# S5 stage: state factors of all batches on VectorE, skip weights put into the inner matrices, turned outputs copied by ScalarE

## The chip, the cores and the metric

The kernel runs on one core of one Trainium2 chip. The metric is the device time of one launch in microseconds (us). A core has TensorE (PE; its weight loads are listed as PEld), VectorE (DVE), ScalarE (ACT), GpSimd (POOL) and SyncE (SP), each with its own instruction stream; the streams meet at semaphores. DMAs are issued here from SP and ScalarE, a few from GpSimd.

## The reference, cut to what matters

The program is two blocks in a row, 512 tokens of width 1024, all in fp32. The first block is a gated linear attention layer and an S5 layer, the second an attention layer with a sparse half and a gated MLP. The change is in the S5 layer:

```python
# s5 mixer, per group g of 16 channels, 64 complex states p
lam_bar = exp(lam * dt); b_bar = (lam_bar - 1) / lam * b
bu[l,g,p] = sum_i u[l,g,i] * b_bar[g,p,i]
states = associative_scan(state[l] = lam_bar * state[l-1] + bu[l])
y = real(states) @ c_re - imag(states) @ c_im
y = y + d_skip * u
y = gelu(y); y = y * sigmoid(y @ w_glu + b_glu); y = y * silu(z)
out = y @ w_out
```

There are 128 groups of 16 channels; u and z are 2048 wide. d_skip (input s5_d, shape 1 x 128 x 16) is the skip weight of every channel.

## The kernel before, in words

Every dense product is made of three TensorE products (high and low parts of weights and activations). The weights come in loads of 1 MB into a ring of three slots, issued by SP (line 2970); ScalarE writes the high part of a load (line 1507), GpSimd (line 2849) or, in the S5 stage, VectorE (`low_weights`, line 2131, "ring_lo") the low part. TensorE takes the tiles in one fixed order, and each engine's order is written out by hand in its own program (`pe_program`, `act_program`, `dve_program`, `pool_program`, `sp_program`).

The S5 layer runs from about 405 to 1000 us. Its scan part works in 16 batches of 8 groups, one after the other. The sequence of 512 tokens is cut in 64 blocks of TB = 8 steps. A batch b needs:

- Bn(b), the input factors, made by VectorE (`b_factors`, lines 2414 to 2417: three instructions on 128 x 1024 elements), which TensorE turns (`b_to_rows`, line 1030, in two halves through one PSUM bank) and ScalarE copies to WB (`b_rows`, line 1739);
- W1(b), the state factors, from the turned C (`c_to_columns`, `columns`, tile CZ). In batches 0 to 10 GpSimd makes them (lines 2889 to 2891), in batches 11 to 15 (`DVE_STATES`) VectorE (`state_factors`, lines 2427 to 2429), again three instructions on 128 x 1024;
- the inner matrix: TensorE's `inside` (line 1041) multiplies Bn and W1, ScalarE's `spread` (line 1747) copies the result to GS, 16 x 8 x 128. Eight DMAs (`inner_rows`, line 2944, by SP; for batch 0 by ScalarE itself, line 1755) lay GS out along the diagonal of KM, a 128 x 1024 matrix whose zeros GpSimd wrote once (line 2882);
- u by blocks: the tile of u goes to DRAM (`u_tile`) and comes back as UB (`u_loads`, eight DMAs by SP);
- TensorE's `additions` (line 1051) multiplies WB and UB, VectorE's `scan` (lines 2449 to 2463) runs the recurrence over the blocks to M;
- TensorE's `outputs` (lines 1062 and 1065) adds UB x KM and M x W1, ScalarE copies (`outputs_of`, line 1762), TensorE turns them back to features (`by_feature`, line 1078, into PA[:, 2]), and VectorE's `add_skip` (line 2403) adds d x u in place into U. ScalarE's `gelu` follows.

Beside each batch TensorE makes dense tiles (`BESIDE`): three in batches 0 to 7 (u and z), two in batches 8 to 15 (z, from batch 10 on the first half of the GLU product, `glu_a`). VectorE scales the u and z tiles (`scaled`, line 2471). In batch 9 VectorE also makes eight low parts of U (line 2080) behind ScalarE's eight high parts.

In the ScalarE program, before the loop over the batches, the order is: `rotations_of(0)`, `u_tile(2)`, `spread(0)` with the eight DMAs of KM[0], `u_tile(3)`; in the loop first `b_rows(b + 1, 0)`. TensorE's second `b_to_rows` of a batch waits until ScalarE has read the first half:

```python
1026:  pe.wait_ge(bf_ready, b + 1)
1027:  if b + h > 0:
1028:      pe.wait_ge(wb_sb, 2 * b + h)
```

SP's stream holds the ring loads and, between them, `inner_rows(b)`, `u_loads(b + 1)` and `factor_loads(b + 3)`, issued when the tile count has reached the batch.

## Time and profile before

| | |
|---|---|
| time, median of 3 runs | 1710.36 us (1709.78 to 1710.69) |
| profiled execution | 1707.65 us, of it the span 1705.8 us |
| mean granted TensorE clock | 0.995 of full speed |
| busy share of the span | PE 98%, PEld 79%, DVE 60%, ACT 40%, POOL 34% |
| chain that ended last, by engine | PE 89%, DVE 6%, ACT 2%, issue 1% |
| TensorE's waits in the S5 stage (420 to 810 us) | 8.1 us in 2 waits for VectorE's Bn; 4.5 us "issue" before outputs (line 1062); 0.3 us for ScalarE's WB |

The busy shares are averages over stages that have different limits. How to read the profile: the table by stretches tells which engine is full in a stretch; the timeline shows an engine's instructions in order, with start, duration, and in brackets the idle time before an instruction and what ended it. A row with "x2" merges instructions; overlapping ends of neighbours come from the pipelines, so the step from one start to the next is the cost in a chain. The profiled execution is 2.7 us below the median of the runs.

### The profile page before, as it was taken

The numbers are of one execution on the slowest core, as the hardware profiler recorded it, in microseconds if no ns is written. First come the engines' busy times: TensorE is split into PE (matmuls) and PEld (weight loads), VectorE is DVE, ScalarE is ACT, GpSimd is POOL, SyncE is SP. The second block draws the span as 40 slices with busy tenths as digits, with TensorE's granted clock in tenths as the row PEclk, the third lists the DMA queues.
The fourth block names the chain that finished last, engine by engine and source line by source line (L and its number), as shares of the span: only waits on it lengthen the run. The fifth ranks groups of instructions, "written<-read, shape, count | busy, mean of one in ns | idle before, by whom it ended". The sixth has DMA issues, their size and how long they took to land.

```text
span 1705.8 us, 23173 instructions
## 1 busy us (share of the span) xinstructions
PE 1672.4 (98%) x9339; PEld 1340.0 (79%) x9339; DVE 1026.0 (60%) x1536; ACT 675.9 (40%) x968; POOL 581.7 (34%) x202
## 2 busy tenths in 40 slices
PE   9999999999999998999999999999999999999998
PEld 7777788888888886777888887687677888887877
DVE  4356535677999999995462755898973222222123
ACT  4473323334443456445333332426673322222122
POOL 2231014343743342000244432233773433443442
PEclk9999999999999999999999999999999999999999
DMA  5232003335645454444744322112002333332322
GB/s 173 75 99 90 10 26 99 85 88 150 158 129 130 137 141 113 115 116 154 265 128 132 99 72 75 50 44 87 1 2 75 98 99 97 82 93 78 100 86 83
DMA packets 266239, 167.86 MB, mean 98 GB/s; under 512 B 88747, under 2 KB 246790, under 8 KB 266006
## 3 DMA queue, kind: packets, MB, share of 16 engines
q1 hardware_dynamic: 254528, 146.44, 30.6%
q10 hardware_dynamic: 11158, 18.08, 3.2%
q0 software_dynamic: 448, 1.88, 0.3%
q8 instruction: 74, 1.21, 0.3%
q14 instruction: 31, 0.25, 0.1%
HBM read 144.86 MB, written 16.78 MB: 95 GB/s over the span
## 4 chain that ended last, share of the span: by engine, by line
PE 89%; DVE 6%; ACT 2%; issue 1%; ACTq 0%; DMA 0%; POOL 0%; DVEq 0%; POOLq 0%
PE PS L726 25%; PE PS L727 24%; PE PS L728 24%; PE PA L1051 1%; PE PA L970 1%; PE PA L967 1%; PE PS L1356 1%; PE PA L944 1%; PE PS L1344 1%; PE PA L1078 1%; PE PA L1306 1%; PE PA L1062 1%; PE PA L1183 1%; DVE ring_lo L2131 1%; PE PS L1030 1%
## 5 line engine op out<-in xcount | busy, mean ns | idle before, releaser
L2849 POOL TENSOR_TENSOR ring_lo<-ring,ring_hi 128x2048 fp32r<-128x2048 f32 (+2 forms) x90 | 393.6, 4373 | 919.2 <-ACT ring_hi L1507 916.6
L1507 ACT ACTIVATE ring_hi<-ring 128x2048 fp32r<-128x2048 f32 (+2 forms) x121 | 220.5, 1827 | 200.8 <-PE PS L728 170.2
L727 PE MATMUL PS<-U3l,ring_hi 128*128 128x512 f32 x352 | 139.9, 397 | 0.0
L726 PE MATMUL PS<-U3h,ring_hi 128*128 128x512 f32 x352 | 139.4, 396 | 0.0
L728 PE MATMUL PS<-U3h,ring_lo 128*128 128x512 f32 x352 | 138.9, 395 | 0.0
L2792 DVE TENSOR_TENSOR SF<-PS,rs 128x512 f32<-128x512 f32 x22 | 15.2, 692 | 162.7 <-PE PS L728 162.7
L726 PE MATMUL PS<-HT5h,ring_hi 128*128 128x512 f32 x256 | 106.9, 418 | 0.0
L2131 DVE TENSOR_TENSOR ring_lo<-ring,ring_hi 128x2048 fp32r<-128x2048 f32 x31 | 92.0, 2980 | 20.2 <-ACT ring_hi L1507 20.0
L728 PE MATMUL PS<-HT5h,ring_lo 128*128 128x512 f32 x256 | 101.7, 397 | 0.0
L727 PE MATMUL PS<-HT5l,ring_hi 128*128 128x512 f32 x256 | 101.5, 397 | 0.0
L2032 ACT ACTIVATE SF<-SF 128x512 f32<-128x512 f32 x22 | 13.9, 632 | 174.2 <-DVE SF L2792 174.2
L2905 POOL TENSOR_SCALAR PB<-PB,mx 128x144 f32<-128x144 f32 (+3 forms) x62 | 69.9, 1139 | 34.5 <-DVE mx L2730 34.5
L726 PEld LDWEIGHTS PS<-U3h,ring_hi 128*128 128x128 f32 x352 | 66.3, 188 | 16.4
L728 PEld LDWEIGHTS PS<-U3h,ring_lo 128*128 128x128 f32 x352 | 66.1, 188 | 16.0
L727 PEld LDWEIGHTS PS<-U3l,ring_hi 128*128 128x128 f32 x352 | 66.2, 188 | 15.2
L726 PE MATMUL PS<-HFh,ring_hi 128*128 128x512 f32 (+1 forms) x198 | 74.3, 375 | 0.9 <-POOL ring_lo L2849 0.9
L727 PE MATMUL PS<-HFl,ring_hi 128*128 128x512 f32 (+1 forms) x198 | 73.2, 370 | 0.0
L728 PE MATMUL PS<-HFh,ring_lo 128*128 128x512 f32 (+1 forms) x198 | 73.2, 369 | 0.0
L726 PE MATMUL PS<-HTh,ring_hi 128*128 128x512 f32 x176 | 70.6, 401 | 1.1 <-ACT QG L1530 1.1
L728 PE MATMUL PS<-HTh,ring_lo 128*128 128x512 f32 x176 | 70.0, 398 | 0.0
L727 PE MATMUL PS<-HTl,ring_hi 128*128 128x512 f32 x176 | 70.0, 398 | 0.0
L2889 POOL TENSOR_TENSOR W<-PW,CZ 128x1024 f32<-128x1024 f32 x11 | 24.7, 2247 | 132.6 <-ACT CZ L1722 117.5
(518 smaller groups left out, 4259.4 us busy)
## 6 DMA issues: line engine op xcount, KB each, us to landing
ring<-in_gla_w_in SPq DMA_DIRECT2D x20, 1024.0 KB, 5.2
ring<-in_s_w_in SPq DMA_DIRECT2D x16, 1024.0 KB, 5.8
ring<-in_s_w_glu SPq DMA_DIRECT2D x16, 1024.0 KB, 5.9
ring<-in_w_gate SPq DMA_DIRECT2D x22, 512.0 KB, 4.0
ring<-in_w_up SPq DMA_DIRECT2D x22, 512.0 KB, 5.2
ring<-in_w_down SPq DMA_DIRECT2D x16, 704.0 KB, 4.5
ring<-in_w_in SPq DMA_DIRECT2D x9, 1024.0 KB, 5.2
ring<-in_gla_w_out SPq DMA_DIRECT2D x8, 1024.0 KB, 5.8
```

The source lines that it names most:

```text
L726: pe.matmul(dst, w[0], x[0], start=start, stop=False)
L727: pe.matmul(dst, w[0], x[1], start=False, stop=False)
L728: return pe.matmul(dst, w[1], x[0], start=False, stop=stop)
L944: pe.matmul(PA[:, (n - 1) % 2, :], KE[r, tt, h * P:(h + 1) * P], V[r, tt, h * GDV:(h + 1) * GDV], start=True, stop=True).then_inc(kv_ps, 1)
L967: m = pe.matmul(dst, V[:, tt, es], ATT[:, h, tt * P:(tt + 1) * P], start=True, stop=False)
L970: m = pe.matmul(dst[:, r], S[:, (c - 1) % 3, es], QG[:, h, c * GCH:(c + 1) * GCH], start=False, stop=c == 2 * tt + 1)
L1030: ins = pe.transpose(PS[:, 1, g * P:(g + 1) * P], Bn[b % 2][:, 4 * h + g, :], ident)
L1507: act.activation(ring_hi[:, n % NSLOT, 0:plan.size[n]], ring[:, n % NSLOT, 0:plan.size[n]], ACT.Copy)\
L2131: tt(ring_lo[:, n % NSLOT, at], ring[:, n % NSLOT, at], ring_hi[:, n % NSLOT, at].bitcast(F32), ALU.subtract).then_inc(wlo_dve, 1)
L2849: pool.tensor_tensor(ring_lo[:, n % NSLOT, at], ring[:, n % NSLOT, at], ring_hi[:, n % NSLOT, at].bitcast(F32), ALU.subtract).then_inc(wlo ...
L2889: link(pool.tensor_tensor(four(W1[b % 3][:]), factor(0, b), rows(CZ[:, p, 0:P]), ALU.mult))
L2905: pool.tensor_scalar(PB[:, n % 6, 0:nk], PB[:, n % 6, 0:nk], mx[:, n % 6, 2:3], None, ALU.mult).then_inc(p_ready, 1)
```

## The change

VectorE makes the state factors of all 16 batches, in the same three instructions; GpSimd only writes the zeros of KM in this part, at its start. The skip term is no longer added to the outputs: a diagonal of the skip weights (DD, made from the identity and DT) is added to the first 16 columns of GS before GS is laid out in KM (`skips`, two instructions on 16 x 128 elements on VectorE), so outputs has it in it. DT, the skip weights with the channel in the partition, is loaded by one DMA from s5_d on SP's queue, ahead of the first u_loads. The DMAs of KM wait for `skip_ready` instead of `gs_ready`. In place of VectorE's add_skip a ScalarE copy (`by_rows`) brings the turned outputs to U.

```diff
--- before.py
+++ after.py
@@ -45,7 +45,6 @@
 BESIDE += [[("glu_a", 2 * j), ("glu_a", 2 * j + 1)] for j in range(6)]
 S5_LAST = [("glu_a", m) for m in range(12, 16)]
 
-DVE_STATES = range(GA + 3, NBATCH)
 
 NM = 16
 T2 = T + NM
@@ -413,6 +412,8 @@
         M_tmp, o = place("M_tmp", [P, BG, NB1], lo + 126 * K1)
         GS, _ = place("GS", [P, BG, P], o)
         YB = sq[:, 0, 0:T]
+
+        DT, DD = sq[0:SGRP, 1, P:2 * P], sq[0:SGRP, 1, 0:P].rearrange("p (g j) -> p g j", g=BG)
         SZ5 = [rs1[:, 0:T], ssq[:, 0:T]]
 
         Z, _ = place("Z", [P, KI, T], lo + 16 * K1)
@@ -522,8 +523,8 @@
         part_in, sig_ready = [sem("part_in0"), sem("part_in1")], sem("sig_ready")
         rs5_used, zs_ready, wr_ready = sem("rs5_used"), sem("zs_ready"), sem("wr_ready")
         small_in = [sem("small_in0"), sem("small_in1")]
-        c_ps, cz_sb, bf_ready, b_ps, wb_sb, w_ready, k_ps, gs_ready, v_ps, m_ready, y_ps, y_sb, yt_ps = (
-            sem("c_ps"), sem("cz_sb"), sem("bf_ready"), sem("b_ps"), sem("wb_sb"), sem("w_ready"), sem("k_ps"),
+        c_ps, cz_sb, bf_ready, b_ps, wb_sb, skip_ready, k_ps, gs_ready, v_ps, m_ready, y_ps, y_sb, yt_ps = (
+            sem("c_ps"), sem("cz_sb"), sem("bf_ready"), sem("b_ps"), sem("wb_sb"), sem("skip_ready"), sem("k_ps"),
             sem("gs_ready"), sem("v_ps"), sem("m_ready"), sem("y_ps"), sem("y_sb"), sem("yt_ps"))
         frac_ready, rot_ready, dk_ready, rot_used, yd_ready, gelu_done = (
             sem("frac_ready"), sem("rot_ready"), sem("dk_ready"), sem("rot_used"), sem("yd_ready"), sem("gelu_done"))
@@ -672,11 +673,7 @@
                 eng.wait_ge(wlo_ready, n + 1 - before)
 
         def states_in(eng, b):
-
-            if b in DVE_STATES:
-                eng.wait_ge(w_dve, b - DVE_STATES.start + 1)
-            else:
-                eng.wait_ge(w_ready, b + 1)
+            eng.wait_ge(w_dve, b + 1)
 
         def fresh(i):
 
@@ -1749,7 +1746,7 @@
                 ins.then_inc(gs_ready, 1)
 
                 if b == 0:
-                    act.wait_ge(gs_ready, 1)
+                    act.wait_ge(skip_ready, 1)
                     act.wait_ge(km_zero, 2)
                     for t in range(TB):
                         act.dma_start(KM[0][t * SGRP:(t + 1) * SGRP, :, t * SGRP:P], GS[0:SGRP, :, 0:P - t * SGRP]).then_inc(km_in[0], 16)
@@ -1761,6 +1758,11 @@
                     act.wait_ge(yt_ps, b)
                 act.activation(YB.rearrange("p (s g i) -> p s g i", s=TB, g=4), PA[:, 0, :].rearrange("p (g s i) -> p s g i", g=4, s=TB),
                                ACT.Copy).then_inc(y_sb, 1)
+
+            def by_rows(b):
+
+                act.wait_ge(yt_ps, b + 1)
+                act.activation(U[:, b, :], PA[:, 2, :], ACT.Copy).then_inc(yd_ready, 1)
 
             def gelu(b):
                 act.wait_ge(yd_ready, b + 1)
@@ -1793,6 +1795,8 @@
                     b_rows(b + 1, 1)
                 if b + 2 < NBATCH:
                     columns(b + 2)
+                if b > 0:
+                    by_rows(b - 1)
                 if b == GA + 1:
 
                     act.wait_ge(gelu_done, GA)
@@ -1817,6 +1821,7 @@
                 tile_out("glu_a", m)
 
             last_out(12)
+            by_rows(NBATCH - 1)
             for b in range(12, NBATCH):
                 gelu(b)
             act.wait_ge(gelu_done, NBATCH)
@@ -2397,11 +2402,6 @@
             def four(ap):
                 return ap.rearrange("p g (s j) -> p g s j", s=TB)
 
-            def add_skip(b):
-
-                dve.wait_ge(yt_ps, b + 1)
-                stt(out=U[:, b, :], in0=U[:, b, :], scalar=pv[:, PV_DS + b:PV_DS + b + 1], in1=PA[:, 2, :], op0=ALU.mult, op1=ALU.add)\
-                    .then_inc(yd_ready, 1)
 
             def b_factors(b, last=lambda: None):
 
@@ -2420,14 +2420,21 @@
             def state_factors(b):
 
                 p = b % 2
-                if b == DVE_STATES.start:
-                    dve.wait_ge(w_ready, b)
-                dve.wait_ge(y_ps, b - 2)
+                if b >= 3:
+                    dve.wait_ge(y_ps, b - 2)
                 dve.wait_ge(cz_sb, b + 1)
                 link(tt(four(W1[b % 3][:]), factor(0, b), rows(CZ[:, p, 0:P].rearrange("p (g j) -> p g j", g=BG)), ALU.mult))
                 link(tt(four(w_tmp[:]), factor(1, b), rows(CZ[:, p, P:2 * P].rearrange("p (g j) -> p g j", g=BG)), ALU.mult))
                 tt(W1[b % 3][:], W1[b % 3][:], w_tmp[:], ALU.add).then_inc(w_dve, 1)
-                dve.wait_ge(w_dve, b - DVE_STATES.start + 1)
+                dve.wait_ge(w_dve, b + 1)
+
+            def skips(b):
+
+                link(tt(DD, con[0:SGRP, C_ID:C_ID + SGRP].unsqueeze(1).broadcast_to([SGRP, BG, SGRP]),
+                        DT[:, b * BG:(b + 1) * BG].unsqueeze(2).broadcast_to([SGRP, BG, SGRP]), ALU.mult))
+                dve.wait_ge(gs_ready, b + 1)
+                tt(GS[0:SGRP, :, 0:SGRP], GS[0:SGRP, :, 0:SGRP], DD, ALU.add).then_inc(skip_ready, 1)
+                dve.wait_ge(skip_ready, b + 1)
 
             def turns(b):
 
@@ -2479,12 +2486,16 @@
             scaled("s5_u", 0)
             low_weights(S5_LOAD + 2)
             scaled("s5_u", 1)
+            state_factors(0)
             link(dve.memset(dk[:].rearrange("p g n -> p (g n)"), 0.0))
             turns(0)
             b_factors(1, lambda: scaled("s5_u", 2))
             scaled("s5_u", 3)
             dve.wait_ge(xt_out, 16)
             link(dve.memset(M[:].rearrange("p g n -> p (g n)"), 0.0))
+            state_factors(1)
+            dve.wait_ge(xt_out, 32)
+            skips(0)
             for b in range(NBATCH):
                 scan(b)
                 own_tiles = [tile for tile in BESIDE[b] if tile[0] != "glu_a"]
@@ -2492,8 +2503,6 @@
                     scaled(*tile)
                 if b + 1 < NBATCH:
                     turns(b + 1)
-                if b > 0:
-                    add_skip(b - 1)
                 if b == GA + 1:
                     scaled(*own_tiles.pop())
                     for i in range(GA):
@@ -2504,11 +2513,11 @@
                     scaled(*tile)
                 if b + 2 < NBATCH:
                     b_factors(b + 2)
-                if b + 2 in DVE_STATES:
                     state_factors(b + 2)
+                if b + 1 < NBATCH:
+                    skips(b + 1)
                 for tile in own_tiles[2:]:
                     scaled(*tile)
-            add_skip(NBATCH - 1)
             dve.wait_ge(y_ps, NBATCH)
             for i in range(GA, KI):
                 low("g", i, U[:, i, :], *fresh(i))
@@ -2854,42 +2863,12 @@
             pool.wait_ge(pw_ready, 1)
             pool.wait_ge(tile_done, tiles["gla_out"][-1].t + 1)
 
-            def factor(i, b):
-                return PW[:, i, :, b * BG:(b + 1) * BG].rearrange("p k g -> p g k").unsqueeze(3).broadcast_to([P, BG, TB, SGRP])
-
-            def rows(ap):
-                return ap.rearrange("p (g j) -> p g j", g=BG).unsqueeze(2).broadcast_to([P, BG, TB, SGRP])
-
-            def four(ap):
-                return ap.rearrange("p g (s j) -> p g s j", s=TB)
-
-            chain = [0]
-
-            def link(ins):
-
-                chain[0] += 1
-                ins.then_inc(pool_chain, 1)
-                pool.wait_ge(pool_chain, chain[0])
-
-            for b in range(DVE_STATES.start):
-                p = b % 2
-                if b == 1:
-
-                    pool.wait_ge(xt_out, 16)
-                    pool.wait_ge(xlo_ready, sum(SPLITS["s5"]))
-                    pool.wait_ge(sq_ready, NORMS["s5"][0] + KD)
-                    for km in KM:
-                        pool.memset(km[:], 0.0).then_inc(km_zero, 1)
-                if b == 0:
-
-                    pool.wait_ge(bf_ready, 1)
-                if b >= 3:
-                    pool.wait_ge(y_ps, b - 2)
-                pool.wait_ge(cz_sb, b + 1)
-                link(pool.tensor_tensor(four(W1[b % 3][:]), factor(0, b), rows(CZ[:, p, 0:P]), ALU.mult))
-                link(pool.tensor_tensor(four(w_tmp[:]), factor(1, b), rows(CZ[:, p, P:2 * P]), ALU.mult))
-                pool.tensor_tensor(W1[b % 3][:], W1[b % 3][:], w_tmp[:], ALU.add).then_inc(w_ready, 1)
-                pool.wait_ge(w_ready, b + 1)
+
+            pool.wait_ge(xt_out, 16)
+            pool.wait_ge(xlo_ready, sum(SPLITS["s5"]))
+            pool.wait_ge(sq_ready, NORMS["s5"][0] + KD)
+            for km in KM:
+                pool.memset(km[:], 0.0).then_inc(km_zero, 1)
             split_weights(tiles["s5_out"][0].loads[0])
             pool.wait_ge(xlo_ready, sum(SPLITS["z"]))
             pool.dma_start(MT[0:NM, :], a["meta_tokens_2"]).then_inc(mt_in, 16)
@@ -2935,7 +2914,7 @@
 
             def inner_rows(b):
 
-                sp.wait_ge(gs_ready, b + 1)
+                sp.wait_ge(skip_ready, b + 1)
                 if b == 1:
                     sp.wait_ge(km_zero, 2)
                 if b >= 2:
@@ -2977,6 +2956,11 @@
                         read_out(sp, tile)
                     sp.dma_start(xt_dram.rearrange("(k p) n -> p k n", p=P), XT[:]).then_inc(xt_out, 16)
                 if n == S5_LOAD + 3:
+
+                    sp.wait_ge(bf_ready, 1)
+                    sp.wait_ge(xt_out, 16)
+                    sp.dma_start(DT, a["s5_d"][0].rearrange("g i -> i g"), allow_slow_non_contiguous=True)\
+                        .then_inc(xt_out, 16)
                     u_loads(0)
                     u_loads(1)
                     factor_loads(2)

```

## Rows read from the trace of the kernel before

**Rows 1.** The page, part 1: busy us, share of the span, instructions

```profile
PE 1672.4 (98%) x9339; PEld 1340.0 (79%) x9339; DVE 1026.0 (60%) x1536; ACT 675.9 (40%) x968; POOL 581.7 (34%) x202
```

**Rows 2.** Stretches: busy us of PE, PEld, DVE, ACT, POOL; PEclk, DMA share, GB/s

```profile
515.00:538.70 23.70, 23.70 (x180) 19.34 (x179) 23.22 (x22) 8.40 (x14) 9.48 (x3) 1.00 0.36 100
...
718.20:737.40 19.20, 18.08 (x156) 14.81 (x156) 18.65 (x21) 9.08 (x16) 0.00 (x0) 1.00 0.52 123
...
684.00:686.00 2.00, 2.00 (x6) 1.61 (x5) 1.93 (x3) 1.07 (x1) 0.00 (x0) 0.50 0.29 66
```

**Rows 3.** VectorE's timeline, batch 11: start us, duration us, engine, line, operation, out<-in, count

```profile
704.94 0.69 DVE L2449 TENSOR_TENSOR M<-PA,rot_c 128x512 f32<-128x512 f32 x1
...
711.92 0.69 DVE L2434 TENSOR_TENSOR rot_c<-r8f,con 128x520 f32<-128x520 f32 x1
...
712.65 0.43 DVE L2212 TENSOR_SCALAR rot_s<-rot_c 128x520 f32<-128x520 f32 x1
...
713.73 0.74 DVE L2403 SCALAR_TENSOR_TENSOR U<-U,pv,PA 128x512 f32<-128x512 f32 x1
...
714.39 2.28 DVE L2131 TENSOR_TENSOR ring_lo<-ring,ring_hi 128x2048 fp32r<-128x2048 f32 x1
...
716.59 1.22 DVE L2414 TENSOR_TENSOR Bn<-PW,BZ 128x1024 f32<-128x1024 f32 x1
...
724.14 0.69 DVE L2449 TENSOR_TENSOR M<-PA,rot_c 128x512 f32<-128x512 f32 x1
```

**Rows 4.** Timeline of TensorE, b_to_rows in batches 9 and 10

```profile
659.38 1.12 PE L1030 MATMUL PS<-con,Bn 128*128 128x128 f32 x4 [3.83 <-DVE Bn L2417]
...
681.98 0.66 PE L1030 MATMUL PS<-con,Bn 128*128 128x128 f32 x4 [4.32 <-DVE Bn L2417]
...
686.82 0.60 PE L1030 MATMUL PS<-con,Bn 128*128 128x128 f32 x4
```

**Rows 5.** Timeline of VectorE before batch 0, beside GpSimd's work

```profile
434.24 2.52 DVE L2212 TENSOR_SCALAR rot_s<-rot_c 128x520 f32<-128x520 f32 x1
...
438.66 2.98 DVE L2415 TENSOR_TENSOR b_tmp<-PW,BZ 128x1024 f32<-128x1024 f32 x1
...
442.28 2.35 DVE L2417 TENSOR_TENSOR Bn<-Bn,b_tmp 128x1024 f32<-128x1024 f32 x1
```

**Rows 6.** VectorE's groups by line, 330 to 425: busy us, mean ns, idle before

```profile
L2341 DVE TENSOR_TENSOR ctmp<-PT 128x128 f32<-128x128 f32 x1 | 0.3, 293 | 0.0
```

**Rows 7.** Timeline of VectorE: scans of batches 8, 9, 10, a tile between

```profile
635.45 0.69 DVE L2449 TENSOR_TENSOR M<-PA,rot_c 128x512 f32<-128x512 f32 x1 [0.99 <-PE PA L1051]
...
659.35 0.69 DVE L2449 TENSOR_TENSOR M<-PA,rot_c 128x512 f32<-128x512 f32 x1
...
670.44 0.69 DVE L2471 TENSOR_TENSOR ssq<-PS,rs 128x512 f32<-128x512 f32 x1 [0.96 <-PE PS L728]
...
685.74 0.69 DVE L2449 TENSOR_TENSOR M<-PA,rot_c 128x512 f32<-128x512 f32 x1
```

**Rows 8.** Timeline around the start of batch 0, three engines

```profile
443.61 1.89 PE L1051 MATMUL PA<-UB,WB 128*128 128x64 f32 x16
...
444.33 5.39 ACTq L1755 DMA_DIRECT2D KM<-GS  x8
...
444.66 0.69 DVE L2471 TENSOR_TENSOR U<-PS,rs 128x512 f32<-128x512 f32 x1
...
445.41 0.49 DVE L2487 MEMSET M<- 128x520 f32 x1
...
447.50 0.60 PE L1030 MATMUL PS<-con,Bn 128*128 128x128 f32 x4
...
451.21 0.63 PE L1030 MATMUL PS<-con,Bn 128*128 128x128 f32 x4 [0.32 <-ACT WB L1739]
```

**Rows 9.** The KM copies that SP issues in batch 12 (715 to 725 us)

```profile
DMA to landing us min/median/max: 3.2/4.4/5.6
```

**Rows 10.** The loads of BZ (line 2925) over the whole run

```profile
DMA to landing us min/median/max: 2.2/2.3/5.6
```

## The prediction, made before the changed kernel was run

> **What bounds the kernel now.** I began with the page's busy line: TensorE works 98% of the span [rows 1]. So a change outside TensorE can only give back TensorE's idle time, or add to it. The diff touches only the S5 stage, so the table by stretches was next, cut at the batches [rows 2]. In the batches with three dense tiles (0 to 7) TensorE is busy 23.70 of 23.70 us, VectorE 23.22 and GpSimd 9.48. In the late ones (10 to 14, two tiles) TensorE is busy 18.08 of 19.20 us and VectorE 18.65. Third, VectorE's timeline of a late batch [rows 3]: from one scan (704.94) to the next (724.14) there is no idle time, and the period is 19.20 us: VectorE bounds these batches. Last, TensorE's rows with a wait [rows 4]: 3.83 us (batch 9) and 4.32 us (batch 10), both for a Bn of VectorE, and after the second the granted clock is 0.50, the 1.2 GHz level [rows 2], in the last row. So three regimes: batches 0 to 7 belong to TensorE, 8 to 14 to VectorE, and what follows to TensorE again.
>
> **Part 1, GpSimd rests.** VectorE's instructions are longer while GpSimd works: rot_s took 2.52 us, against 0.43 us for the same instruction in late batches; b_tmp 2.98 and the last step of Bn 2.35, against 1.23 us for such an instruction [rows 3, 5]. The memsets of KM stay on GpSimd; they now come right after the XT write has landed, before anything waits for them.
>
> **Part 2, state factors on VectorE.** Six linked instructions, Bn and W, take 7.55 us from 716.59 to 724.14, so three take 3.78 us [rows 3]. It is added to batches 0 to 10.
>
> **Part 3, skips for add_skip.** add_skip held VectorE for 714.39 - 713.73 = 0.66 us. skips is two instructions of 16 x 128 elements. The nearest row is a 128x128 product, 0.29 us [rows 6]; with 0.04 us for the link behind each (three of 1.22 take 3.78 from start to start) two take 0.66 us. No row has 16 partitions; below, the smallest could be nearly free, above, twice this. I take 0.66: a late batch keeps its period of 19.20.
> The turned outputs now go through ScalarE, one copy a batch, ahead of outputs_of, where ScalarE has idle time; from TensorE's side it only replaces one reader of PA by another.
>
> **Batches 0 to 7.** VectorE's work is scan and turns 8.79 (704.94 to 713.73), three tiles at 0.61, one or two ring_lo at 2.20 (714.39 to 716.59), Bn and W 7.55, skips 0.66: 21.0 or 23.2 us, under TensorE's 23.7. After the second tile, which is TensorE's to give, 0.61 + 7.55 + 0.66 + 0.61 = 9.4 us follow; in the same place now VectorE ends and still waits 0.99 us for the additions [rows 7]. I find it level with them, and what scan makes is used only after the second tile. Cost nothing. inner_rows on SP's queue waits for skips instead of gs_ready, up to some 10 us later by my estimate; behind it stand u_loads, factor_loads and the next ring load, all used a batch or so later. Cost nothing; without that cover, 1 to 2 us.
>
> **The start of batch 0.** Here I find the loss. ScalarE issues the eight KM[0] DMAs itself, and waits for skip_ready first. Behind them on ScalarE stand u_tile(3) and b_rows(1, 0), and TensorE's second b_to_rows waits for that b_rows. From the first KM issue (444.33) to TensorE's transposes (451.21) is 6.88 us, and TensorE already waits 0.32 us there [rows 8]. When can skips(0) be done? VectorE's order is now: u tile 3, memset M, state_factors(1), skips(0). It reached u tile 3 at 444.66. Before it, state_factors(0) adds 3.78, and the three stretched instructions lose 2.09 + 1.75 + 1.12 = 4.96 [rows 3, 5], so 443.5 at the latest; others shrink too, but the tile itself ends about 0.7 us before the additions at 443.61 [rows 8], as three products stand between. I take 443.0. Scaling and memset 1.24 (444.66 to 445.41 and 0.49), state factors 3.78, skips 0.66: 448.7. TensorE then goes on at 448.7 + 6.88 = 455.6, against 451.21: **+4.35 us**. It stands still for almost 4.9 us. After the wait of 4.32 us its two b_to_rows were 686.82 - 681.98 = 4.84 us apart [rows 4], where at full clock, in batch 0, they are 451.21 - 447.50 - 0.32 = 3.39 apart [rows 8]: a clock loss of about 1.5 us. Bounds 0 and 2; I take **+1.5**. As batches 1 to 7 are TensorE's, all 5.85 us go on to batch 8; and VectorE waits for TensorE's additions at scan 8, so it starts 5.85 late as well.
>
> **Batches 8 to 14.** Scan 8 to scan 9 took 659.35 - 635.45 = 23.90 us [rows 7]. Without GpSimd: 8.79 + two tiles 1.22 + two ring_lo 4.40 + 7.55 + 0.66 = 22.62, a gain of **1.28**. Scan 9 to scan 10 took 26.39 us, with 0.96 of waiting for a tile [rows 7]. W was already VectorE's there; TensorE's tile now comes in time, but ScalarE's eight high parts gate the eight low parts, and the new copy stands before them. Bounds of the gain 0 and 0.96, I take **0.3**. Batches 10 to 13: 0. The inner matrices of batch b are now copied only after skips(b), which ends as scan b starts: eight issues in 5.4 us (ScalarE's in [rows 8]), so the last one begins 4.7 us after the first, and a KM copy lands at the least 3.2 us after its issue, behind a ring load [rows 9]: up to 7.9 us, against scan's 6.98 (704.94 to 711.92). Now that no ring load is just ahead, I expect it level with the scan: 0, up to 1.5 us, and only once, since TensorE's idle 1.1 us a batch takes the rest.
>
> **The sum.** +4.35 + 1.5 - 1.28 - 0.3 = **+4.3 us**. The profiled execution took 1707.65 us (span 1705.8 and 1.85 around it), so 1712.0 for it; the median of the runs is 1710.36, 2.7 above the profiled one, and gives **1714.7**.
>
> **Rivals.**
> **A, the forecast**, chance 0.60: TensorE stalls once in batch 0, +4.3. Its own range is from no clock loss and a stall a microsecond shorter (+1.8) to a second cost of 1.5 at the KM copies and 1 us more of stall (+6.9): 1712 to 1717.5. For it: order of ScalarE's instructions in code and the 0.32 us wait, which shows no slack. Of the 0.60, 0.18 lie within 0.2%.
> **B, the wait at the start is covered**, 0.18: only -1.28 - 0.3 is left, 1708.8. It decides if skips(0) ends by about 444; against it is the 3.78 us of state factors behind u tile 3.
> **C, the load of the skip weights comes late**, 0.12. It reads s5_d across its rows, so 2048 runs of 4 bytes, ahead of the UB loads on the same queue. BZ, with 512 runs of 64 bytes, landed in 2.2 to 5.6 us, median 2.3 [rows 10]. Four times the worst is 22 us from about 431: 453.4, 5.4 us after VectorE is ready for it (448.0), and everything moves by as much: 1720.1. It costs only what is over 17 us. By four times the median, 9 us, it costs nothing, and I think that likelier.
> **D, faster**, 0.10: the batches bounded by VectorE shrink. Place: VectorE's 19.20 us of batches 8 to 13. If the 16-partition instructions cost only 0.15 us each, six batches give 6 x 0.36 = 2.2 us; it ends on the other side only if the stall of A is absent too: 1710.36 - 1.58 - 2.2 = 1706.6. Decides from skips at 0.35 us a batch and skips(0) before 444.
>
> The Trainium skill, page DMA: Bandwidth & Descriptors, section Rules for kernel authors, speaks against the new load: it says that a strided last dimension becomes one descriptor per element and should be rearranged. No run here has shown such a load; by that rule alone C would be more likely, and the sum by it is up to 1720.1 as worked out above.
>
> **Range and chances.** 1708.5 to 1719.5: it takes in A, nearly all of B and the smaller part of C; outside are D and the end of C. A measurement of this kernel can tell about 0.2%, 3.4 us. Faster 0.10 (D); within 0.18 (A) + 0.18 (B) = 0.36; slower 0.42 + 0.12 = 0.54. The likeliest case alone: 1712 to 1717.5.
>
> **What would show it.** After: the KM[0] issues on ScalarE begin at about 448.7 and TensorE's second b_to_rows near 455.6, with a wait of 4 to 5 us on ScalarE's WB and granted clock 0.5 behind it; no wait before Bn in batch 9 any more, one in batch 10; late batches still 19.2 us apart with VectorE never idle; VectorE's 1024-element products all at 1.2 us; skips of two 0.3 us instructions. Wrong would be: a TensorE wait on KM in late batches (a period above 19.2), a wait for the skip load before 448, or no wait in batch 0 at all.

## The result, and the profile of the changed kernel

The changed kernel took 1714.3 us (median of 12 runs, 1713.2 to 1714.9), the kernel before, in runs beside it, 1709.7 us (12 runs, 1708.1 to 1710.7). The ratio is 1.0029, with a 95% interval of 1.0021 to 1.0036: 0.29% slower. The forecast was 1714.7 us, with slower as the likeliest sign.

The profiled execution of the changed kernel took 1714.28 us, its span is 1712.5 us. TensorE is as full as before, GpSimd has 107 us less to do (33 instructions fewer), VectorE's busy time falls although it has 49 instructions more [rows 1]. First the page, part 1 of the changed kernel (busy us, share of the span, instructions):

```profile
PE 1677.0 (98%) x9339; PEld 1342.8 (78%) x9339; DVE 1016.8 (59%) x1585; ACT 683.2 (40%) x984; POOL 474.8 (28%) x169
```

Then TensorE's waits from 420 to 820 us, the S5 batches (us in total, times, longest us). Before, the same view had the two waits for Bn, 8.1 us together, 4.5 us of "issue" before outputs, and only 0.3 us for WB:

```profile
PE PS L1027 <- ACT WB L1736: 4.7, 1, 4.7
PE PA L1059 <- DMA KM<-GS: 4.1, 4, 1.3
PE PS L1027 <- DVE Bn L2417: 3.7, 1, 3.7
PE PA L1048 <- issue: 1.7, 1, 1.7
PE PA L1059 <- issue: 0.6, 1, 0.6
```

One wait for Bn has gone (batch 9) and one for ScalarE's WB has come. It lies at the start of batch 0; the timeline there, three engines, answers to [rows 8]. To lay it over the rows of before, 1.24 us must be added to each time: the additions of batch 0 began at 442.37 here and at 443.61 before. Where the 1.24 us come from is only in part known: before had a slow stretch of the granted clock near 240 us, worth 1.7 us, which this execution did not have, but the second trace of the changed kernel (c_after) had it too and its additions began at 442.53.

```profile
443.21 1.22 DVE L2426 TENSOR_TENSOR W<-PW,CZ 128x1024 f32<-128x1024 f32 x1
...
446.99 0.28 DVE L2433 TENSOR_TENSOR sq<-con,sq 16x128 f32<-16x128 f32 x1
447.30 0.28 DVE L2436 TENSOR_TENSOR GS<-GS,sq 16x128 f32<-16x128 f32 x1
447.62 5.29 ACTq L1752 DMA_DIRECT2D KM<-GS  x8
...
452.95 0.60 ACTq L1690 DMA_DIRECT2D u_by_block<-U  x1
453.66 0.60 ACT L1736 ACTIVATE WB<-PS 128x512 f32<-128x512 f32 x1 [11.86 <-issue]
...
454.40 0.91 PE L1027 MATMUL PS<-con,Bn 128*128 128x128 f32 x4 [4.75 <-ACT WB L1736]
```

Read it as a chain: VectorE makes the state factors of batch 1 (three products from 443.21), then the two short instructions of skips(0); only then may ScalarE issue the eight copies of KM[0], which hold it for 5.29 us; behind them stand u_tile(3) and b_rows(1, 0), whose WB TensorE's second b_to_rows needs. TensorE waits 4.75 us, against 0.32. What the clock did is in the table of stretches (us, busy us of PE, PEld, DVE, ACT, POOL; PEclk, DMA share, GB/s):

```profile
451.00:455.50 4.50, 1.10 (x7) 1.13 (x7) 4.36 (x7) 1.84 (x2) 0.00 (x0) 0.90 1.56 194
455.50:457.00 1.50, 1.50 (x6) 1.21 (x5) 1.43 (x3) 1.50 (x2) 0.00 (x0) 0.50 1.42 238
457.00:459.00 2.00, 2.00 (x8) 1.56 (x7) 2.00 (x2) 1.62 (x3) 0.00 (x0) 0.74 0.27 103
```

Behind the wait TensorE is busy all the time, at 0.50 of its full clock, the 1.2 GHz level. The scans of VectorE, which answer to [rows 3, 7]:

```profile
640.21 0.69 DVE L2456 TENSOR_TENSOR M<-PA,rot_c 128x512 f32<-128x512 f32 x1
...
654.48 0.69 DVE L2478 TENSOR_TENSOR ssq<-PS,rs 128x512 f32<-128x512 f32 x1 [0.39 <-PE PS L725]
...
663.26 0.69 DVE L2456 TENSOR_TENSOR M<-PA,rot_c 128x512 f32<-128x512 f32 x1
...
689.11 0.69 DVE L2456 TENSOR_TENSOR M<-PA,rot_c 128x512 f32<-128x512 f32 x1
...
708.29 0.69 DVE L2456 TENSOR_TENSOR M<-PA,rot_c 128x512 f32<-128x512 f32 x1
...
727.48 0.69 DVE L2456 TENSOR_TENSOR M<-PA,rot_c 128x512 f32<-128x512 f32 x1
```

Scan 8 to 9 is 23.05 us (before 23.90), 9 to 10 25.85 (26.39), a late batch 19.19 (19.20). The table sets the two traces and those of the experiments side by side, each time from the additions of batch 0, so that what lies ahead of them drops out; "rest" is what follows scan 15, where TensorE's instructions are the same in all of them. All values are differences of starts in the timelines, in us.

| kernel | outputs(0) | scan 8 | 8 to 9 | 9 to 10 | 10 to 15 | scan 15 | rest |
|---|---|---|---|---|---|---|---|
| before | 12.59 | 191.84 | 23.90 | 26.39 | 91.94 | 334.07 | 928.1 |
| after | 18.59 | 197.84 | 23.05 | 25.85 | 91.88 | 338.62 | 931.5 |
| c_after | 18.95 | 198.20 | 23.04 | 25.86 | 91.83 | 338.93 | 930.1 |
| e1_skips_first | 13.37 | 192.61 | 23.05 | 25.84 | 91.86 | 333.36 | 928.3 |
| e2_km_sync | 13.15 | 192.40 | 23.05 | 25.84 | 91.85 | 333.14 | 928.2 |
| e3_both | 12.64 | 191.88 | 23.05 | 25.84 | 91.85 | 332.62 | 928.3 |
| e4_states_only | 12.07 | 191.31 | 22.60 | 25.21 | 91.92 | 331.04 | 929.7 |
| e5_skips_only | 15.53 | 194.78 | 23.92 | 27.67 | 91.84 | 338.21 | 929.8 |
| e6_filler | 17.47 | 196.72 | 23.05 | 25.84 | 91.84 | 337.45 | 928.2 |
| e7_skips_early | 12.90 | 192.15 | 23.05 | 25.85 | 91.85 | 332.90 | 931.3 |
| e9_lows_gpsimd | 12.07 | 191.31 | 22.61 | 26.08 | 103.71 | 343.71 | 930.9 |
| e10_angles_act | 12.07 | 191.32 | 22.42 | 25.21 | 89.01 | 327.96 | 930.1 |
| e11_product_first | 12.47 | 191.71 | 22.73 | 25.54 | 91.85 | 331.83 | 929.7 |
| e12_dt_late | 19.41 | 198.65 | 23.05 | 25.85 | 91.85 | 339.40 | 929.8 |

The change costs 338.62 - 334.07 = 4.55 us in the batches. The spans differ by 6.7: 4.55, less 1.24 ahead of the batches, plus 931.5 - 928.1 = 3.4 behind them, which is slow clock too, as the last section shows.

### The profile page after: what moved, and what is told of

Its sections match the earlier page's. It is cut to its first block, busy times and chain, and to the rows that moved or that the text cites. A ratio compares the mean times of both kernels' runs of the same rounds, so it can differ in the third digit from the quotient of the medians.

```text
span 1712.5 us, 23222 instructions
## 1 busy us (share of the span) xinstructions
PE 1677.0 (98%) x9339; PEld 1342.8 (78%) x9339; DVE 1016.8 (59%) x1585; ACT 683.2 (40%) x984; POOL 474.8 (28%) x169
## 4 chain that ended last, share of the span: by engine, by line
PE 86%; DVE 9%; ACT 2%; issue 1%; DMA 0%; ACTq 0%; SPq 0%; POOL 0%; DVEq 0%; POOLq 0%
PE PS L723 24%; PE PS L724 23%; PE PS L725 23%; PE PA L967 1%; PE PA L964 1%; PE PS L1353 1%; PE PA L941 1%; PE PS L1341 1%; DVE ring_lo L2136 1%; PE PA L1048 1%; PE PA L1303 1%; PE PA L1180 1%; PE PA L1059 1%; PE PA L1075 1%; PE PA L1062 1%
## 5 line engine op out<-in xcount | busy, mean ns | idle before, releaser
L2136 DVE TENSOR_TENSOR ring_lo<-ring,ring_hi 128x2048 fp32r<-128x2048 f32 x31 | 70.5, 2287 | 19.5 <-ACT ring_hi L1504 19.3
L723 PE MATMUL PS<-U2hf,ring_hi 128*128 128x512 f32 (+2 forms) x176 | 64.3, 366 | 0.2 <-ACT RL L1909 0.2
```

Source lines behind the costliest of these rows:

```text
L723: pe.matmul(dst, w[0], x[0], start=start, stop=False)
L2136: tt(ring_lo[:, n % NSLOT, at], ring[:, n % NSLOT, at], ring_hi[:, n % NSLOT, at].bitcast(F32), ALU.subtract).then_inc(wlo_dve, 1)
```

## Experiments at the start of batch 0: is it ScalarE's wait?

Three theories stood against each other. S: the loss is ScalarE's wait for skips(0), with b_rows(1, 0) queued behind the copies. V: it is VectorE's larger load, wherever it stands. G: the stall is real but is given back in batches 8 to 10, where TensorE waits for VectorE anyway.

**e1_skips_first** exchanges two steps of VectorE in the changed kernel.

```diff
-            state_factors(1)
             dve.wait_ge(xt_out, 32)
             skips(0)
+            state_factors(1)
```

> The changed kernel with one step moved: VectorE makes skips(0) before state_factors(1), so ScalarE's KM[0] issues can begin 3.78 us earlier (at about 443.8 instead of 447.62 in the trace after). Theory S (ScalarE's wait for the skips, with b_rows(1, 0) queued behind it, is the loss): TensorE's wait on WB in batch 0 falls from 4.75 to about 1.0 us, granted clock stays at 1.00 there, the time falls by 3.8 to 5.2 us, from 1714.3 to 1709.1 to 1710.5. Rival V (the loss is VectorE's larger load, not its order): the work is the same, so nothing moves, 1714.3. Rival G (the stall is real but its cost is taken back in batches 8 to 10, where TensorE waits for VectorE anyway): the stall is gone, the time stays within 1 us of 1714.3.

1707.15 us (10 runs, 1706.1 to 1712.0), ratio to before 0.9992, interval 0.9980 to 1.0003. The timeline of ScalarE and TensorE:

```profile
444.20 5.41 ACTq L1752 DMA_DIRECT2D KM<-GS  x8
...
450.36 0.60 ACT L1736 ACTIVATE WB<-PS 128x512 f32<-128x512 f32 x1 [8.14 <-issue]
...
451.10 0.63 PE L1027 MATMUL PS<-con,Bn 128*128 128x128 f32 x4 [1.10 <-ACT WB L1736]
```

The copies begin 3.78 us earlier against the additions (1.47 behind them, in place of 5.25), the wait is 1.10 us, and outputs(0) comes at 13.37 in place of 18.59. Same instructions, other order: V falls, and as scan 15 moves by the same 5.26 us (338.62 to 333.36), G falls too. The median fell by 7.15 us, more than the 3.8 to 5.2 expected: the rest behind the batches is shorter as well, 928.3 us against 931.5.

**e2_km_sync** leaves VectorE's order as it is and takes the copies from ScalarE.

```diff
-                if b == 0:
-                    act.wait_ge(skip_ready, 1)
-                    act.wait_ge(km_zero, 2)
-                    for t in range(TB):
-                        act.dma_start(KM[0][...], GS[...]).then_inc(km_in[0], 16)
...
-                if b >= 1:
-                    inner_rows(b)
+                inner_rows(b)
```

> The changed kernel, but batch 0's inner matrices are issued by SyncE, as in every other batch, instead of ScalarE; VectorE's order is untouched. Theory S: ScalarE has no wait in front of b_rows(1, 0), so the 4.75 us wait of TensorE and the slow clock behind it are gone; the KM issues begin at about 447.8 on SyncE, the last lands near 456.3, and outputs(0), wanted at about 455.0, waits some 1.3 us. The time falls by 4.5 to 6 us, to 1708.3 to 1709.8. Rival V: nothing moves, 1714.3. Rival G: within 1 us of 1714.3.

1708.57 us (10 runs), ratio 0.9995 (0.9986 to 1.0005). TensorE has no wait on WB; its first outputs now wait 1.01 us for the copies:

```profile
446.81 0.60 ACT L1736 ACTIVATE WB<-PS 128x512 f32<-128x512 f32 x1 [5.09 <-PE PS L1027]
...
447.83 5.20 SPq L2917 DMA_DIRECT2D KM<-GS  x8
...
455.44 0.44 PE L1059 MATMUL PA<-KM,UB 128*64 128x128 f32 x4 [1.01 <-DMA KM<-GS]
```

**e3_both** exchanges the two steps and lets ScalarE issue four of the copies and SyncE four.

```diff
-                    for t in range(TB):
+                    for t in range(4):
                         act.dma_start(KM[0][...], GS[...]).then_inc(km_in[0], 16)
...
-                for t in range(TB):
+                for t in range(4 if b == 0 else 0, TB):
```

> The changed kernel with skips(0) before state_factors(1), four of the KM[0] copies issued by ScalarE and four by SyncE. Theory S: neither b_rows(1, 0) nor outputs(0) waits, so only the gains in batches 8 and 9 (0.85 and 0.54 us) are left against the kernel before: about 6 us under the changed kernel, 1708.3. Rival V: 1714.3. Rival G: within 1 us of 1714.3.

1707.45 us (10 runs), ratio 0.9990 (0.9980 to 0.9999). outputs(0) at 12.64 is where it was before (12.59), and scan 15 is 1.45 us earlier than before, which is 0.85 + 0.55 for batches 8 and 9 and 0.09 in late ones, less 0.04 at the start. So the delay at the start of batch 0 is this one wait and what follows from it, and without it the changed kernel is 0.1% below the one before, at the edge of the interval (1708.3 us had been expected). It is not all that skips costs: against e4 below, which has no skips, scan 15 of e3 is still 1.58 us late (332.62 and 331.04).

**e6_filler** asks what the slow clock behind the wait costs: 18 products that nobody reads, in the wait.

```diff
                 dense(*beside[0], 4, KD)
+                if b == 0:
+                    for _ in range(18):
+                        pe.matmul(PA[:, 2, :], HT5h[:, 0, 0:P], HT5h[:, 0, :], start=True, stop=True)
                 if b + 1 < NBATCH:
                     b_to_rows(b + 1, 1)
```

> The changed kernel with 18 products whose result nobody reads (128 x 512, 0.235 us each, 4.2 us) on TensorE ahead of its second b_to_rows in batch 0, so inside the wait of 4.75 us. Theory of the clock term: the wait ends where it did (454.4 in the trace after), but the granted clock stays 1.00 behind it, and outputs(0) comes about 1.5 us earlier: 1712.8. Rival (the slow clock there costs nothing on the path): 1714.3, outputs(0) at the same distance from additions(0), 18.6 us. If the fillers last longer than the wait, more than 1714.3.

1710.45 us (10 runs). TensorE's timeline, and the clock behind the wait:

```profile
450.38 4.27 PE L1106 MATMUL PA<-HT5h 128*128 128x512 f32 x18
455.76 0.63 PE L1027 MATMUL PS<-con,Bn 128*128 128x128 f32 x4 [1.11 <-ACT WB L1739]
```

```profile
455.50:457.00 1.50, 1.24 (x9) 1.19 (x10) 1.47 (x4) 1.50 (x2) 0.00 (x0) 1.00 1.81 91
457.00:459.00 2.00, 2.00 (x10) 1.61 (x9) 1.97 (x3) 2.00 (x2) 0.00 (x0) 1.00 0.89 262
```

With the engine kept busy the granted clock stays at 1.00. From b_to_rows to outputs(0) it is now 460.74 - 455.76 = 4.98 us, in the changed kernel 460.96 - 454.40 = 6.56, before 456.20 - 451.21 = 4.99: the slow clock costs 1.57 us in this trace. Two more traces with the same wait give 1.87 (c_after, 6.85 us) and 2.15 (e12, 7.13 us), so it is a figure of one execution. As WB came 0.46 us later here (12.49 behind the additions, in place of 12.03), 1.12 of it is seen at outputs(0). The median fell by 3.85 us, more than that; the rest behind the batches differs too (928.2 us against 931.5), of which below. That is also why it is under the 1712.8 expected.

**e12_dt_late** tests rival C of the prediction: the load of the skip weights is issued behind the UB loads.

```diff
-                    sp.dma_start(DT, a["s5_d"][0].rearrange("g i -> i g"), allow_slow_non_contiguous=True)
...
                     u_loads(0)
                     u_loads(1)
+                    sp.dma_start(DT, a["s5_d"][0].rearrange("g i -> i g"), allow_slow_non_contiguous=True)
...
```

> The changed kernel with the load of the skip weights issued behind the 16 UB loads, at about 441.7 instead of 429.46; at its landing time of 7.8 us it is there at 449.5, 2.5 us after VectorE is ready for it (447.0). Theory of rival C of the prediction (the load is free up to 17 us and costs one for one beyond): TensorE's wait on WB in batch 0 grows from 4.75 to about 7.3 us and the time to 1716.8. Rival (VectorE's start of batch 0 has slack): 1714.3. If the load takes longer behind the UB loads than alone, more than 1716.8.

1714.41 us (10 runs), the same as the changed kernel; the 1716.8 expected did not come. The load landed 4.0 us after its issue at 440.9, so at 444.9, before VectorE asked for it (447.98); in the changed kernel it took 7.8 us from 429.46. TensorE's wait was 5.00 us, not 7.3, and outputs(0) came 0.82 later than in the changed kernel, of which 0.57 is the slow clock just named. So the load never was late in any run here, and what it costs when it is was not reached: rival C is excluded for this kernel, its price beyond that point is untested.

## Experiments on the parts: what did the moved work bring?

**e4_states_only** is the kernel before with the state factors of all batches on VectorE, GpSimd idle, and add_skip where it was.

```diff
-DVE_STATES = range(GA + 3, NBATCH)
+DVE_STATES = range(0, NBATCH)
...
             scaled("s5_u", 1)
+            state_factors(0)
...
             link(dve.memset(M[:].rearrange("p g n -> p (g n)"), 0.0))
+            state_factors(1)
```

> The kernel before with one part of the change alone: VectorE makes all state factors, GpSimd rests, the skip stays where it was (add_skip; no skips, no copy on ScalarE). Theory S with the contention term: no stall at batch 0, since ScalarE's KM[0] issues wait only for its own copies; VectorE's stretched instructions are gone; batch 8 gives about 0.9 and batch 9 about 0.5 us back: 1708.3 against 1709.7. Rival V (VectorE's load is the loss): most of the 4.6 us appears here, about 1714. Rival N (GpSimd's work never cost anything on the path): 1709.7, and scan 8 to scan 9 stays at 23.9 us.

1705.73 us (10 runs), ratio 0.9985 (0.9975 to 0.9994). This half of the change by itself is a gain of 3.03 us in the batches: 0.53 up to scan 8, 1.30 in batch 8, 1.18 in batch 9. I had expected 0.9 and 0.5 in the two batches, what the changed kernel showed there; that they are larger says that the other half takes something back.

**e5_skips_only** is the kernel before with the other half: skips and ScalarE's copy in place of add_skip, the state factors of batches 0 to 10 on GpSimd.

```diff
-                if b > 0:
-                    add_skip(b - 1)
...
+                if b + 1 < NBATCH:
+                    skips(b + 1)
...
-                    act.wait_ge(gs_ready, 1)
+                    act.wait_ge(skip_ready, 1)
```

> The kernel before with the other part of the change alone: skips (and the copy on ScalarE) in place of add_skip; GpSimd keeps the state factors of batches 0 to 10. Theory S: ScalarE's KM[0] issues wait for skips(0), which here follows u tile 3 and the memset of M directly: 444.66 + 0.75 + 0.49 + 0.63 = 446.5 in the frame of the trace before, against 444.33, so TensorE's wait there grows from 0.32 to about 2.5 us, with up to 1.5 us of slow clock; and by the theory of places (add_skip stood ahead of VectorE's wait for a dense tile and filled it, skips stands behind it) batches 8 and 9 become up to 1.1 us longer: together +2 to +5 us, 1711.5 to 1714.5. Rival (skips costs nothing but its 0.63 us, which add_skip took too, and the loss needs the state factors in front of it): 1709.3 to 1709.8.

1713.52 us (10 runs), ratio 1.0024 (1.0015 to 1.0034). It loses 4.14 us in the batches: the copies begin 3.74 behind the additions in place of 0.72, so outputs(0) is 2.94 late (at a granted clock of 1.00: its wait is 3.3 us), and batch 9 is 1.28 longer. The wait was expected at 2.5. What was missing is that GpSimd, at work on the state factors of batch 1, held the first instruction of skips(0), which took 1.07 us in place of 0.28:

```profile
442.27 3.24 POOL L2905 TENSOR_TENSOR W<-W,w_tmp 128x1024 f32<-128x1024 f32 x1
...
444.58 1.07 DVE L2439 TENSOR_TENSOR sq<-con,sq 16x128 f32<-16x128 f32 x1
```

Batch 8 is only 0.02 longer, since VectorE has no wait there with GpSimd beside it. Of the 1.28 in batch 9, 0.63 is skips behind the wait for the tile; the other 0.66 is the tile, which TensorE gives that much later, at a slow clock (its two b_to_rows are 5.88 us apart there, 4.59 before).

The halves sum to -3.03 + 4.14 = +1.1, together they gave +4.55. Of the 3.4 between them, 3.6 arise up to scan 8 (-0.53 and +2.94 against +6.00) and 0.15 is given back behind it. The 3.6 are three parts: the copies begin 1.51 us later than in e5 (5.25 behind the additions, in place of 3.74), the slow clock of 1.57 comes only with the longer wait, and the 0.53 that e4 had won is not had. The state_factors(1) ahead of skips(0) take 3.78 us, but against e5 only 1.51 of it shows, as VectorE, beside GpSimd's work, was 2.26 us later there.

**e11_product_first** looks at the 0.45 and 0.63 us by which batches 8 and 9 are longer with skips than in e4. add_skip stood ahead of VectorE's wait for a dense tile, skips stands behind it. The edit, on e3, takes the first product of skips out, as products(b), and calls it at that place.

```diff
                 if b + 1 < NBATCH:
                     turns(b + 1)
+                    products(b + 1)
```

> The kernel e3 with the first of the two instructions of skips (0.31 us, it needs nothing of its batch) moved up to where add_skip stood, ahead of VectorE's wait for the second dense tile. Theory of places: that product goes into the wait of batch 8 (0.39 us) and the wait on the high parts in batch 9 (0.57 us), so scan 8 to 9 falls from 23.05 to 22.74 and scan 9 to 10 from 25.84 to 25.53; late batches, which have no wait, stay at 19.17. Rival (the 0.45 and 0.63 us that skips costs there against the states alone come from ScalarE's copy or from the longer path to the inner matrices): both distances stay as they are.

One run, 1706.16 us. VectorE's timeline:

```profile
643.88 0.27 DVE L2433 TENSOR_TENSOR sq<-con,sq 16x128 f32<-16x128 f32 x1
...
657.21 0.69 DVE L2459 TENSOR_TENSOR M<-PA,rot_c 128x512 f32<-128x512 f32 x1
...
667.86 4.91 DVE L2085 TENSOR_TENSOR UAl<-U,UAh 128x512 fp32r<-128x512 f32 x8 [0.25 <-ACT UAh L1518]
...
682.75 0.69 DVE L2459 TENSOR_TENSOR M<-PA,rot_c 128x512 f32<-128x512 f32 x1
```

Batches 8 and 9 take 22.73 and 25.54 (expected 22.74 and 25.53), late ones as before; the wait for the high parts is 0.25 us in place of 0.57. Here an instruction of 0.3 us costs nothing ahead of a wait and 0.3 us behind it.

**e7_skips_early**, on e3, makes skips(b + 1) ahead of state_factors(b + 2), because TensorE waited for the KM copies four times in the changed kernel.

```diff
                     b_factors(b + 2)
-                    state_factors(b + 2)
                 if b + 1 < NBATCH:
                     skips(b + 1)
+                if b + 2 < NBATCH:
+                    state_factors(b + 2)
```

> The kernel e3 with skips(b + 1) moved ahead of state_factors(b + 2) in every batch, so the inner matrices are copied 3.78 us earlier. Theory (the KM copies gate TensorE's outputs in late batches, but VectorE's own 19.17 us per batch is the bound): TensorE's 3.9 us of waits on KM in 3 batches disappear, the scans stay 19.17 us apart, additions(0) to scan 15 stays at 332.6 us: no gain, 1707. Rival (the waits for KM cost time): up to 3.9 us less, additions(0) to scan 15 near 329.

One run, 1709.09 us. TensorE's waits from 405 to 820 us:

```profile
PE PS L1027 <- DVE Bn L2417: 6.9, 1, 6.9
PE PA L1059 <- issue: 4.8, 5, 1.3
PE PA L1059 <- DMA KM<-GS: 0.5, 1, 0.5
```

The waits for KM shrink from 3.9 us (in e3) to 0.5, those marked "issue" at the same line (the profile shows nothing that TensorE waited for) grow from 1.6 to 4.8, and the batches take the same time: 332.90 us against 332.62. The name of a wait is not its cost: outputs needs the end of the scan as well, and the kernel before waited there too, 4.5 us in four batches, under the name "issue". Its batch 11 comes first, then batches 11 and 12 of the changed kernel:

```profile
712.11 0.44 PE L1062 MATMUL PA<-KM,UB 128*64 128x128 f32 x4 [0.94 <-issue]
```

```profile
715.60 0.44 PE L1059 MATMUL PA<-KM,UB 128*64 128x128 f32 x4 [0.77 <-DMA KM<-GS]
...
734.64 0.44 PE L1059 MATMUL PA<-KM,UB 128*64 128x128 f32 x4 [0.92 <-DMA KM<-GS]
```

From the start of the scan to outputs it is 7.17 us before, and 7.31 and 7.16 in the changed kernel. So of the 4.1 us of waits put down to KM the copies held outputs for 0.14 us, once; in e3 and c_after it was 0.5, also in batch 11 alone (7.64 and 7.68). e7 takes that 0.5 away (7.17) and gains nothing, so the rival falls, though it was a half microsecond that was tested and not 3.9.

**e9_lows_gpsimd**, on e4, gives the idle GpSimd the low weight parts of batches 9 to 15.

```diff
+    POOL_LOWS = range(LOWS[9].start, LOWS[NBATCH - 1].stop)
+    DVE_LOADS = [n for n in DVE_LOADS if n not in POOL_LOWS]
...
                 for n in LOWS[b]:
-                    low_weights(n)
+                    if n not in POOL_LOWS:
+                        low_weights(n)
```

> The kernel with the state factors alone on VectorE (1705.7), and GpSimd, now idle, makes the low weight parts (ring_lo) of batches 9 to 15 in place of VectorE. Theory of contention (from batch 3 of before: 9.48 us of GpSimd went with about 6.5 us of longer instructions on VectorE, 0.69 us for each): 4.6 us of GpSimd cost VectorE 3.2 us, more than the 2.29 us it is spared, so late batches go from 19.2 to about 20.1 us: 5 us slower, 1710.5. Rival (GpSimd beside VectorE is free for this instruction): the period falls to TensorE's 18.1 to 18.3, 6 to 8 us faster, 1698 to 1700.

1719.18 us (4 runs, 1717.5 to 1724.9), ratio 1.0066 (1.0045 to 1.0087). A late batch takes 21.2 us (723.22 to 744.45), and this is where:

```profile
726.12 1.24 DVE L2459 TENSOR_TENSOR_SCAN M_tmp<-M,dk 128x520 f32<-128x520 f32 x1
726.41 5.34 POOL L2853 TENSOR_TENSOR ring_lo<-ring,ring_hi 128x2048 fp32r<-128x2048 f32 x1 [15.15 <-ACT ring_hi L1509]
...
727.39 4.93 DVE L2462 TENSOR_TENSOR M<-M_tmp,rot_s 64x520 f32<-64x520 f32 x1
```

The scan, which had begun before GpSimd, keeps its 1.24 us; the instruction behind it takes 4.93 us in place of 0.70 and ends 0.57 us after GpSimd does (726.41 + 5.34 = 731.75). VectorE is spared 2.29 us and held for 4.23. I had expected 3.2, from the share of the earlier batches, so contention was right and its size too small: 1719.2 us in place of 1710.5. Of the 12.7 us that e9 loses against e4 up to scan 15, 5.7 are in batch 14, which had time to spare in e4 (15.1 us, now 20.8). The Trainium skill, page SBUF — State Buffer, section SBUF: two separate sides, says that the port pair which VectorE and GpSimd share is "an exclusive lock, not a bandwidth split"; by that rule an instruction caught by it waits for the other's end, and this trace agrees, with the 4.93 us.

**e10_angles_act**, on e4, gives ScalarE the first product of turns, as eight instructions with a scale by partition, ahead of outputs_of, in all batches but batch 9.

```diff
+            def angles(b):
+                act.wait_ge(m_ready, b)
+                for g in range(BG):
+                    ins = act.activation(rot_c[:, g, :], con[:, C_NI:C_NI + NB1], ACT.Copy,
+                                         scale=r8f8[:, 1, b * BG + g:b * BG + g + 1])
+                ins.then_inc(pool_chain, 1)
...
+                if b in ANGLES:
+                    dve.wait_ge(pool_chain, ANGLES.index(b) + 1)
```

> The kernel with the state factors alone on VectorE (1705.7), and the first product of turns (0.73 us of VectorE from start to start) made by ScalarE in eight small instructions, in its gap ahead of outputs_of, in all batches but one. Theory (VectorE's chain of instructions is the whole period of batches 8 to 14): scans of late batches come 18.45 us apart instead of 19.20, six times, so 4.4 us faster: 1701.3. Rival (ScalarE's eight instructions hold up its YB copy and the spread, or TensorE's 18.1 us of work with its waits takes over): the period stays above 18.8, and no more than 2 us are gained.

1702.41 us (4 runs, 1702.3 to 1702.7), ratio 0.9960 (0.9945 to 0.9975): faster than both kernels.

```profile
718.57 0.69 DVE L2462 TENSOR_TENSOR M<-PA,rot_c 128x512 f32<-128x512 f32 x1
...
725.66 2.03 ACT L1740 ACTIVATE rot_c<-con,r8f 128x65 f32<-128x65 f32 x8 [3.27 <-DVE M L2476]
...
737.04 0.69 DVE L2462 TENSOR_TENSOR M<-PA,rot_c 128x512 f32<-128x512 f32 x1
```

A late batch takes 18.47 us, as the theory said (18.45); the sum was too large, 3.08 us in the batches in place of 4.4, because it counts in batches 10 to 13 alone (4 x 0.73): batch 14, which makes no more factors, took 15.1 us in both, batch 8 gave 0.18, and batch 9 was left out.

**c_after** is the changed kernel unchanged, once more.

> The changed kernel itself once more, as a control for the part of the trace behind the S5 batches. Theory: additions(0) to scan 15 is 338.6 us again, within 0.1, as it depends on the code; the slow stretches of the granted clock behind it (at 1005 and 1070 us in the trace after) are tied to where the program stands, since kernels with the same instructions there show the first one or not by kernel: it is there again and the time is 1714.3. Rival (they fall by chance from run to run): the trace shows fewer of them, and single times scatter by 1.7 us steps between 1710.9 and 1714.3.

1713.87 us (10 runs), ratio 1.0027 (1.0017 to 1.0037). The batches took 338.93 us, 0.3 more than in the first trace, not within 0.1; most of it is the slow clock behind the wait, 1.87 us here. So differences under 0.4 us between two traces up to scan 8 are not to be read. Behind the batches the first slow stretch is there again, as the theory said, but the second is shorter (rest 930.1 us, in place of 931.5), which the theory did not allow; the distances from scan 8 on repeat within 0.02 (10 to 15: within 0.05).

## Why the prediction was right, point by point

- **Start of batch 0, forecast +4.35: 4.43.** With the 1.24 us added, the KM[0] issues begin at 448.86 (said: 448.7) and b_to_rows at 455.64 (455.6). TensorE's wait grew from 0.32 to 4.75 us. e1, e2 and e3 show that it is the queue on ScalarE. That batches 1 to 7 neither add to the delay nor take it back was right too: outputs(0) and scan 8 are both 6.00 us later (forecast 5.85). The step that found it is the order of ScalarE's instructions behind the first issue [rows 8], with VectorE's new load put in front of it. That VectorE would not reach the tile later was sound as well: the stretched instructions of [rows 5] are 0.43, 1.23 and 1.22 us now.
- **Clock, forecast +1.5: 1.57**, by e6. It was read [rows 4] behind another stall, of 4.32 us. That it came so close is partly luck: the same wait cost 1.87 and 2.15 us in two other traces, and behind e5's wait of 3.3 us there was no slow clock at all.
- **Batch 8, forecast -1.28: -0.85.** This term was mis-sized, and e4 says why: without skips the batch gives 1.30 us. The mechanism of part 1 was right; what failed is the step of part 3 that set 0.66 us of skips against 0.66 of add_skip. The durations were right (0.63 us from start to start for the two), but only equal places make equal costs: add_skip stood ahead of a wait for TensorE's tile and skips behind it. With add_skip gone VectorE came to the tile early and waited 0.39 us for it, and skips was paid behind it.
- **Batch 9, forecast -0.3: -0.54.** e4 gives -1.18 for the state factors alone, beyond my upper bound of 0.96: the wait for the tile [rows 7] counts 1.04 us from start to start, and the low parts behind it had waited another 0.12. With skips 0.63 is lost again, because where add_skip (0.66) stood VectorE now waits 0.57 us idle, 0.66 from start to start, for ScalarE's high parts, and the two instructions of skips come on top. The two errors partly made up for each other.
- **Late batches, forecast 0: -0.06** (91.94 to 91.88).
- **KM copies, forecast 0, up to 1.5 once: 0.** The profile puts 4.1 us of TensorE's waits down to them, in four batches, but they end with the scan as the forecast had it ("level with the scan"): outputs is held by 0.14 us, once. The sign of being wrong that the prediction named, a wait on KM in late batches, was not a good one, as the wait of before stood in the same place under another name; the period beside it, 19.2 us, was.
- **Rivals.** B (the wait is covered) falls with the 4.75 us. C falls with the load's 7.8 and 4.0 us. The Trainium skill, page DMA: Bandwidth & Descriptors, section Rules for kernel authors, advises against such a load, as the prediction told; no run shows its descriptors, and the trace shows that its 7.8 us were hidden here. D needed 0.15 us for each 16 x 128 instruction; they take 0.28.
- **The sum, +4.3: 4.55** between additions(0) and scan 15. The forecast of the median, 1714.7 against 1714.3, is luck in part. For the profiled execution the sum gave 1712.0 us, and it took 1714.3: 0.3 more in the batches and 3.4 behind them, less 1.24 ahead. Neither of the last two was forecast. The +2.7 from profile to median, which I had added, made up for them; in the changed kernel profile and median are the same. Over more runs the median of before was 1709.3 to 1710.0.

## What to carry to other kernels

A step that a change puts ahead of a DMA issue delays all that its engine has queued behind the issues: 3.8 us of products on VectorE, and the 0.6 of skips, became 4.4 us of standing on TensorE, and 1.6 more at the slow clock, though VectorE and ScalarE had time to spare in these batches. In a region bounded by one engine, ask of each of its instructions on which side of its waits it stands: ahead of one it is free up to the wait's length (shown here for 0.3 us). Ask of a wait what else the instruction needs, and when that came, before you read its name as a cost. Try the parts of a change alone: one half of this one was worth 3 us, and with the other half it was a loss.
